# Attention hand-offs and the bias table in a gated decoder block: bias spread by two heads, one mix read later, turned blocks through PSUM, one value product a step later

## What is computed

```python
h = rms_norm(x, pre_norm[l])
proj = h @ w_in[l]
q, k, v, gate_a, u_b, v_b, gate_b, mg_a, mg_b = jnp.split(proj, offsets, axis=-1)
o_a = sliding_window_attention(q, k, v, sinks[l], rel_bias)      # reshaped to heads
y_a = (o_a * jax.nn.silu(gate_a)) @ w_branch_a[l]
o_b = spatial_gating(gelu(u_b), gelu(v_b), ...)   # u * (tril(W_s) LN(v) + b)
y_b = (o_b * jax.nn.silu(gate_b)) @ w_branch_b[l]
merged = jax.nn.sigmoid(mg_a) * y_a + jax.nn.sigmoid(mg_b) * y_b
x = x + rms_norm(merged @ w_out[l], post_norm[l])
```

## Time and profile before

| | us |
|---|---|
| median of 3 runs | 909.6 |
| lowest and highest of them | 908.57, 911.26 |
| the profiled execution | 908.92 |
| its span, first to last instruction | 907.2 |

### The profile page before, as it was taken

How to read it: one execution, slowest core, us unless ns; L and a number is a source line. 1 busy time by engine, 2 the same in 40 slices (tenths; PEclk the granted TensorE clock), 3 DMA queues, 4 the chain that set the end, 5 groups by cost and what they waited for, 6 DMA issues and landing times.

```text
span 907.2 us, 12749 instructions
## 1 busy us (share of the span) xinstructions
PE 894.8 (99%) x4268; PEld 746.9 (82%) x4268; DVE 671.5 (74%) x1167; ACT 500.9 (55%) x982; POOL 498.2 (55%) x395
## 2 busy tenths in 40 slices
PE   9999999999999999999999989999999999999997
PEld 7888788888888888888888868888888888888886
DVE  6766695576666666757576669688689878989968
ACT  6554254775767676666767664334443434534563
POOL 3564235777787777787869636445542252043236
PEclk9999999999999999999999999999999999999999
DMA  8788764433434346534343443533289550435004
GB/s 311 194 201 241 240 209 105 136 104 86 134 88 127 95 117 163 150 105 117 102 116 103 116 146 105 186 117 123 62 292 334 185 209 1 139 114 211 1 1 185
DMA packets 170512, 130.90 MB, mean 144 GB/s; under 512 B 58552, under 2 KB 139472, under 8 KB 170320
## 3 DMA queue, kind: packets, MB, share of 16 engines
q1 hardware_dynamic: 168208, 126.66, 45.7%
q10 hardware_dynamic: 2240, 3.43, 1.2%
HBM read 93.87 MB, written 39.35 MB: 147 GB/s over the span
## 4 chain that ended last, share of the span: by engine, by line
PE 84%; DVE 5%; ACT 4%; issue 3%; SPq 2%; DMA 1%; POOL 0%; DVEq 0%; POOLq 0%; ACTq 0%
PE acc L1019 42%; PE acc L1200 11%; PE ps_m L1200 7%; PE ps_t L1200 7%; PE acc L872 7%; PE ps_t L1036 2%; PE acc L962 2%; PE ps_m L1067 2%; SPq L506 1%; ACT prob L1570 1%; DVE neg_s L2137 1%; DVE pt_pack L2151 1%; ACT prob L1578 1%; DVE ps_t L2134 1%; PE ps_t L1046 1%
## 5 line engine op out<-in xcount | busy, mean ns | idle before, releaser
L1019 PE MATMUL acc<-mv,w_hi 128*128 128x512 f32 x1344 | 353.8, 392 | 0.0
L1019 PEld LDWEIGHTS acc<-mv,w_hi 128*128 128x128 f32 x1344 | 244.8, 188 | 44.9
L1019 PE MATMUL acc<-mv,w_lo 128*128 128x512 f32 x672 | 182.0, 393 | 0.0
L1813 POOL TENSOR_TENSOR w_lo<-sums,w_hi 128x1024 fp32r<-128x1024 f32 x48 | 118.0, 2460 | 73.1 <-ACT w_hi L1366 48.9
L1019 PEld LDWEIGHTS acc<-mv,w_lo 128*128 128x128 f32 x672 | 126.7, 189 | 28.6
L1813 POOL TENSOR_TENSOR w_lo<-raw,w_hi 128x1024 fp32r<-128x1024 f32 (+1 forms) x48 | 95.2, 1984 | 40.1 <-ACT w_hi L1359 32.6
L1570 ACT ACTIVATE prob<-neg_s,neg_max 128x129 f32<-128x129 f32 x128 | 50.5, 396 | 89.7 <-DVE neg_max L2137 89.6
L1200 PE MATMUL acc<-right,left 128*128 128x512 f32 x432 | 98.7, 389 | 0.0
L1200 PEld LDWEIGHTS acc<-right,left 128*128 128x128 f32 x432 | 81.0, 188 | 17.2 <-DVE left L2203 0.4
L2151 DVE TENSOR_TENSOR pt_pack<-turned_in,pt_pack 128x256 fp32r<-128x256 f32 x32 | 43.6, 1362 | 42.5 <-ACT pt_pack L1588 42.5
L1857 POOL TENSOR_SCALAR_AFFINE_SELECT pt_prev<-pt_pack 128x512 fp32r<-128x512 f32 x64 | 40.8, 638 | 58.6 <-DVE pt_pack L2127 39.8
(11 more groups left out here) (286 smaller groups left out, 1688.0 us busy)
## 6 DMA issues: line engine op xcount, KB each, us to landing
raw<-in_w_in SPq DMA_DIRECT2D x56, 512.0 KB, 4.5
ht_d<-sums SPq DMA_DIRECT2D x8, 512.0 KB, 4.9
mix_d<-mix_b SPq DMA_DIRECT2D x8, 512.0 KB, 4.0
prob_d<-prob SPq DMA_DIRECT2D x32, 128.0 KB, 2.2
turned_in<-prob_d SPq DMA_DIRECT2D x128, 32.0 KB, 2.2
ga_d<-gate SPq DMA_DIRECT2D x16, 256.0 KB, 4.1
tb<-tb_d SPq DMA_DIRECT2D x4, 1024.0 KB, 5.1
ub<-mix_d SPq DMA_DIRECT2D x7, 512.0 KB, 3.4
```

The lines of the kernel that those rows point to most:

```text
L1019: ins = nc.tensor.matmul(bank, (w_lo if y == 2 else w_hi)[:, left + k * P:left + (k + 1) * P], right[:, (OPW if y == 1 else 0) + k * HALF: ...
L1813: nc.gpsimd.tensor_tensor(w_lo[:, c], src, w_hi[:, c].bitcast(f32), ALU.subtract).then_inc(wlo_ok, 1)
```

## The change

There are four edits.

1. The bias table is spread by two heads at a time: at t = 5 ScalarE issues the DMA of head pair 0 alone, and SyncE issues that of head pair p + 1 at k = 7 of head pair p. `load_bias(p)` waits for its own part.
2. In U pair 16 `u_mix` and the first `u_mul` stand at s = 5 in place of s = 3 and s = 4.
3. For even blocks ScalarE copies `turned_in` as it is into `ps_q`, the free quarter of `ps_t`, and VectorE makes both parts from there by the function `cast`, which odd blocks use as well. `ps_q` and `ps_p` lie in one PSUM bank. The copy waits until the odd block before it is split (`ptl_ok`, 2j + 1), and the transpose of an odd block waits until the **even** block before it is split too (`place - 1` in place of `place - 2`).
4. The value product of odd blocks stands at k = 6, 9, 12, 15 in place of 5, 8, 11, 14.

```diff
-        ps_s, ps_p = ps_t[:, 0:512], ps_t[:, 512:768]
+        ps_s, ps_p, ps_q = ps_t[:, 0:512], ps_t[:, 512:768], ps_t[:, 768:1024]
...
+        def skew(p):
+
+            return (skew_d[2 * p:2 * p + 2, :, :],
+                    bass.AP(bias_d, 2 * p * BIAS_ROW, [[BIAS_ROW, 2], [0, P], [1, BIAS_ROW]]))
...
             def load_bias(p):
-                if p == 0:
-                    sp.wait_ge(bias_out, 32)
-                else:
+                sp.wait_ge(bias_out, 32 + 16 * p)
+                if p:
                     sp.wait_ge(scores_used, 8 * p)
...
+                if k == 7 and p + 1 < HEAD_PAIRS:
+                    sp.dma_start(*skew(p + 1)).then_inc(bias_out, 16)
                 if k == 11 and p + 1 < HEAD_PAIRS:
                     load_bias(p + 1)
...
                 if s > 1:
-                    pe.wait_ge(ptl_ok, place(p, blk) - 2)
+                    pe.wait_ge(ptl_ok, place(p, blk) - 1)
...
-                for blk in odd_at(k, 5) + even_at(k, 7):
+                for blk in odd_at(k, 6) + even_at(k, 7):
                     values(p, blk)
...
-                    act.dma_start(skew_d[:, :, :], bass.AP(bias_d, 0, [[BIAS_ROW, N_HEADS], [0, P], [1, BIAS_ROW]])).then_inc(bias_out, 16)
+                    act.dma_start(*skew(0)).then_inc(bias_out, 16)
...
-            def turned_hi(p, blk):
+            def turned_copy(p, blk):
                 j = 4 * p + blk // 2
                 act.wait_ge(prob_in, 64 * (j + 1))
-                if j:
-                    act.wait_ge(values_ok, 2 * j)
-                else:
-                    act.wait_ge(v_out, 16)
-                nc.scalar.activation(pt_pack[0][:, 0:256], turned_in[:, :], ACT.Copy).then_inc(turn_hi, 1)
+                act.wait_ge(ptl_ok, 2 * j + 1)
+                nc.scalar.activation(ps_q, turned_in[:, :], ACT.Copy).then_inc(turn_in, 1)
...
+            def cast(p, blk, src):
+
+                if place(p, blk) > 2:
+                    dve.wait_ge(values_ok, place(p, blk) - 2)
+                else:
+                    dve.wait_ge(v_out, 16)
+                pack = pt_pack[blk % 2]
+                own.link(nc.vector.tensor_copy(pack[:, 0:256], src))
+                nc.vector.tensor_tensor(pack[:, 256:512], src, pack[:, 0:256].bitcast(f32), ALU.subtract).then_inc(ptl_ok, 1)
...
                 for blk in even_at(k, 5):
-                    dve.wait_ge(turn_hi, 4 * p + blk // 2 + 1)
-                    pack = pt_pack[0]
-                    nc.vector.tensor_tensor(pack[:, 256:512], turned_in[:, :], pack[:, 0:256].bitcast(f32),
-                                            ALU.subtract).then_inc(ptl_ok, 1)
+                    dve.wait_ge(turn_in, 4 * p + blk // 2 + 1)
+                    cast(p, blk, ps_q)
...
-                    if kind(n) == "U" and n < PAIRS - 1:
+                    if FIRST_U < n < PAIRS - 1:
                         u_mix(n)
...
-                    if kind(n) == "U":
+                    if n > FIRST_U:
                         u_mul(n, 0)
...
+                if s == 5 and n == FIRST_U:
+                    u_mix(n)
+                    u_mul(n, 0)
```

More of the change, by code:

```diff
@@ L300, in build @@
         sink_ok = sem("sink_ok")
-        turn_ok, prob_out, prob_in, turn_hi = sem("turn_ok"), sem("prob_out"), sem("prob_in"), sem("turn_hi")
+        turn_ok, prob_out, prob_in, turn_in = sem("turn_ok"), sem("prob_out"), sem("prob_in"), sem("turn_in")
         pt_done, ptl_ok, pt_ok, values_ok = sem("pt_done"), sem("ptl_ok"), sem("pt_ok"), sem("values_ok")
@@ L1595, in attend @@
                 for blk in even_at(k, 5):
-                    turned_hi(p, blk)
+                    turned_copy(p, blk)
                 if k in (8, 11, 14, 17):
@@ L2118, in attend @@
                 for blk in odd_at(k, 3):
-                    s = 8 * p + blk
-                    dve.wait_ge(pt_done, s // 2 + 1)
-                    if s == 1:
-                        dve.wait_ge(v_out, 16)
-                    else:
-                        dve.wait_ge(values_ok, place(p, blk) - 2)
-                    pack = pt_pack[1]
-                    own.link(nc.vector.tensor_copy(pack[:, 0:256], ps_p))
-                    nc.vector.tensor_tensor(pack[:, 256:512], ps_p, pack[:, 0:256].bitcast(f32), ALU.subtract).then_inc(ptl_ok, 1)
+                    dve.wait_ge(pt_done, (8 * p + blk) // 2 + 1)
+                    cast(p, blk, ps_p)
                 for blk in blocks_at(k, 0):
```

## The result

The changed kernel takes 920.89 us in the median, the kernel before 910.78 on the same chip. The ratio is 1.0105, with a 95% interval from 1.0083 to 1.0127. One of the six executions took 1822.21 us; it was a slow one, which the ratio leaves out, and the median of the other five is 920.71 us. The forecast was 909.6, from 903.5 to 914.0: the changed kernel is about 10 us slower than before, and 7 us beyond the end of that range.

What follows compares the result with a forecast made beforehand. TensorE, busy 894.8 of 907.2 us, was taken as the bound. Gains of 6.9 us against 7.0 paid gave a 907.3 us span; adding 1.7 and 0.7 it forecast 909.6 us, range 903.5 to 914.0.

Steps and rivals of the forecast that it cites:

- the k = 6 payment: At k = 6 TensorE's transpose newly waits for the even block's split: 0.87 us in each of eight head pairs, 7.0 us.

Runs made afterwards that it cites:

- e8: Changed kernel with the bias spread's 128 rows outermost and ScalarE's copy of each head pair's first three even blocks a step earlier: 901.08 us, ratio 0.9906.
- a2: The changed kernel measured again, unaltered, against the kernel before: 919.99 us, ratio 1.0113.
- e2: Changed kernel with the bias of all 16 heads spread by one DMA again, other three edits kept: 910.25 us, ratio 0.9998.
- e3: Kernel before with only the even blocks' copy into PSUM and split by VectorE added: 917.69 us, ratio 1.0090.
- e7: Kernel before with only the odd blocks' value products moved a step later: 910.13 us, ratio 0.9998.
- e5: Kernel before with only the bias spread by two heads, outermost dimension 2: 920.50 us, ratio 1.0118.
- e1: Changed kernel with the two-head bias spread's outer dimensions swapped, 128 rows outermost: 907.84 us, ratio 0.9977.
- e4: Kernel before with two-head bias spread (128 rows outermost), later first mix and later odd value products, without the copy into PSUM: 901.92 us, ratio 0.9916.

## What to carry to other kernels

When a transfer is cut into pieces, look at what is left in its outermost dimension before scaling its time by its bytes: a piece of two entries ran on two of 16 DMA engines here, each with as many bytes to move as in the whole, and a swap of two dimensions gave 12 us back. Cost a DMA that is put into a queue by what stands behind it there, down to that transfer's readers and their slack, not only by its own reader. And where an instruction newly waits for another engine, read how the two stand against each other before the change: that gave the k = 6 payment, 6.7 to 7.0 us against the 7.0 forecast, and showed in e8 where to move the copy so that nothing is paid.

## What the runs showed of the hardware

- A DMA from DRAM to DRAM with an outermost dimension of 2, 4 (two in a row) and 128 moved 384 KB at some 50 GB/s, at some 100 GB/s, and too fast to be told from the transfers beside it, with DMA shares of 0.13, 0.27 and more. Two, four and sixteen of the completion increments of one such DMA came with its data. A 128 KB write behind it on the same queue landed 10.0, 7.0 and 4.0 us after its issue, and 2.2 without it; two, four and none of its sixteen increments were cut off from the others.
- Late starts of TensorE of up to 1.8 us (after the first ten microseconds) were followed by starts at the usual pitch; behind those of 2.1 (a2), 2.65 (e2), 3.5 (before) and 4.8 us (e3) products of 512 columns started 0.427 us apart, at 1.2 GHz. The length of the wait alone doesn't decide it: starts 2.64 us late in e7 and 3.60 us late in e5 were followed by the usual pitch at a granted clock of 1.00, and behind a start of 3.5 to 3.6 us the clock of ten microseconds was 0.83 in before and 0.66 in e7. So a wait longer by 1.4 us (e2 against before, at 100 us) could make 2.8 us in the time, and the kernel before, with a wait of varying length at 100 us and one of 3.5 at 531, scatters over 4.5 us, where e1, e4 and e8, without both, stay within 0.6.
- ScalarE's copy of 128x256 into PSUM took 0.36 us in a free stretch, 0.39 behind a DMA, and 0.40 into SBUF.
